# Order of the last row sums and a middle result in PSUM, in a two-layer decoder trunk on one core

## The chip, the core and the metric

The kernel runs on one core of a Trainium2 chip. The time is that of the device in microseconds (us), the median over runs of the whole kernel. The engines are named as in the profile: PE (TensorE), DVE (VectorE), ACT (ScalarE), POOL (GpSimd) and SP (SyncE, which here only issues DMAs).

## The reference, cut to what matters

```python
# 512 tokens of 1024 numbers, 2 layers; all in float32
for i in range(2):
    m = short_conv_mixer(x, ...) if i == 0 else chunked_sgu_mixer(x, ...)
    x = layer_norm(ALPHA * x + m, ln_mix_g[i], ln_mix_b[i])
    f = grouped_moe(x, ...)          # 16 experts, 2 for each token, both from one group of 4
    x = layer_norm(ALPHA * x + f, ln_ffn_g[i], ln_ffn_b[i])

def layer_norm(x, g, b):             # over the 1024 numbers of a token
    mu, var = mean(x), mean((x - mu) ** 2)
    return (x - mu) * rsqrt(var + 1e-5) * g + b
```

The change lies in the last two lines of the second layer: the sum of a token's own row with its two expert rows, and the norm of that sum, which is the output. A small part of it is in the routing of both layers, where the tokens of each expert are counted.

## The kernel before, in words

**Tiles.** The 512 tokens stand as four tiles of 128 tokens (`t` = 0 to 3), one token to a partition, 1024 numbers along it. `X[:, t, :]` in SBUF holds a tile. PSUM has 8 banks of 512 float32 numbers a partition (`ps[:, bank, :]`), so a tile takes two banks. `SB[1] = (2, 4, 0, 6)` names the first of the two banks in which the sums of tiles 0 to 3 are built in the second layer; `summed(t)` is the pair of them.

**Experts.** Each of 16 experts gets up to 112 token rows. The weights stream from HBM all the time; ACT and DVE split each into a rounded part `hi` (L466) and a rest `lo` (L477), and PE multiplies in three passes (L481 to L483). The outputs of the first 14 experts are scattered to a table `y_rows` in HBM by an indirect DMA that POOL issues (L556). The table has two halves, one for each of a token's two experts. When it is written, POOL issues for tiles 1 to 3 a DMA that adds the first half's rows to `X` (L959, semaphore `first_in`), and, as each of these lands, one that adds the second half's rows (L963, semaphore `second_in`). Tile 0 is read by SP and added by DVE.

**The last two experts** don't go through the table. Their outputs stay in SBUF, as `y_last` (two experts, a `hi` and a `lo` part each), and PE brings each row to its token by a product with a one-hot matrix `hotT`. `sum_half(1, t, h)` (L2086) does it for half `h` (512 numbers) of tile `t`: 4 products, so 8 for a tile. `own_rows(t, h)` (L2099) then adds `X`'s own rows to the same bank, by a product with the identity in full float32; the trace shows each call as two products, so 4 for a tile. It needs `second_in[t]`, since `X` is complete only then. Before the change PE works tile by tile: the one-hot products of the tile, the wait for its `second_in`, its own rows. Each call of `own_rows` raises `sum_ready`.

**The norm of a tile** (tiles 1 to 3) on DVE: two `bn_stats` from PSUM (L1638), each after its half's `sum_ready`; `bn_aggr` for mean and variance (L1360); `(sum - mean) * gain` from PSUM to `X` (L1366); the reciprocal `rstd` of the root that ACT took meanwhile (L1370). For tiles 0 to 2 DVE stops there: ACT multiplies `X` by `rstd` (L1204), POOL adds the bias (L984), and SP sends the tile out (L876). For tile 3, the last, DVE itself does `X * rstd + bias` in two halves (L1378); ACT sends the first half out (L1225), SP the second (L878). DVE's instructions run in the order in which they are written, tile after tile, and so do those of PE, ACT, POOL and SP.

**The counts.** `counts(layer)` (L1904) sums the tokens of each expert into 16 columns of PSUM bank `LGB[layer]`, which is 4 in the first layer and 2 in the second; `route_most` (L1466) takes the largest. Every engine reads it later, and runs further rounds of all experts only if it is over 112.

Of the kernel before, what the change touches and what calls it, by code (L numbers as in the profile page):

```python
# [33 lines left out]
AX = mybir.AxisListType  # L34
# [4 lines left out]
NT = S // P  # L39
KD = D // P  # L40
BANK = 512
E = 16
# [125 lines left out]
def hybrid_decoder(nc, x, x_t, w_dense0, w_moe, w_dense1, conv_w, router_w, router_bias,  # L168
                   w_s, b_s, v_gain, v_bias, ln_par, out):
    ctx = ExitStack()  # L170
    with ctx:
# [24 lines left out]
        X = place("X", [P, NT, D], F32, 80 * KB)  # L196
# [18 lines left out]
        ffn_par = [place(f"ffn_par{l}", [P, 2, D], F32, o) for l, o in ((0, 72 * KB), (1, 40 * KB))]  # L215
# [31 lines left out]
        ones_b = place("ones_b", [P, P], BF16)  # L247
# [28 lines left out]
        rstd = place("rstd", [P, NT], F32)  # L276
# [9 lines left out]
        sel = place("sel", [P, NT, E], BF16, bsb_at)  # L286
# [45 lines left out]
        scr = [scratch(0), scratch(1)]  # L332

        ps = ctx.enter_context(nc.psum_tensor("ps", [P, 8, BANK], F32))
# [152 lines left out]
        TRF = (2, 4, 0, 0)  # L487
        SB = ((2, 4, 0, 2), (2, 4, 0, 6))
        LGB = (4, 2)
        IDA = (7, 3)  # L490
        NA = 3

# [786 lines left out]
        def _(dve):  # L1279
            chain = Chain(dve, dve_step)  # L1280
# [79 lines left out]
                nc.vector.bn_aggr(mv[:, t, :], stats[:, :, :].rearrange("p a b -> p (a b)")).then_inc(var_ready, 1)  # L1360
                dve.wait_ge(var_ready, q + 1)

            def norm(q, t, par, n_par, last_step=True, src=None, parts=1):

                dve.wait_ge(par_in, 32 * n_par)
                chain.step(nc.vector.scalar_tensor_tensor(out=X[:, t, :], in0=X[:, t, :] if src is None else src,  # L1366
                                                          scalar=mv[:, t, 0:1], in1=par[:, 0, :],
                                                          op0=ALU.subtract, op1=ALU.mult))
                dve.wait_ge(std_ready, q + 1)
                ins = nc.vector.reciprocal(rstd[:, t:t + 1], std[:, t:t + 1])  # L1370
                if not last_step:
                    ins.then_inc(rooted, 1)
                    return
                chain.step(ins)
                n = D // parts
                for c in range(parts):
                    cols = slice(c * n, (c + 1) * n)
                    nc.vector.scalar_tensor_tensor(out=X[:, t, cols], in0=X[:, t, cols], scalar=rstd[:, t:t + 1],  # L1378
                                                   in1=par[:, 1, cols], op0=ALU.mult, op1=ALU.add).then_inc(normed, 1)

            def mixed(layer, t):
# [81 lines left out]
            def route_most(layer):  # L1463

                dve.wait_ge(cnt_ready, layer + 1)
                chain.step(nc.vector.reduce_max(scr[layer]["most_f"][:, :], ps[:, LGB[layer], 192:192 + E], axis=AX.X))  # L1466
                nc.vector.tensor_copy(most[:, layer:layer + 1], scr[layer]["most_f"][:, :]).then_inc(most_ready, 1)

            def route_gates(layer):
# [129 lines left out]
            def combine(layer):  # L1599

                def x_lo(t):
                    for h in range(2):
                        dve.wait_ge(xt_hi, 4 + 2 * t + h + 1)
                        dst = slice(4 * h, 4 * h + 4), slice(t * P, (t + 1) * P)
                        nc.vector.tensor_tensor(xT_lo[:, dst[0], dst[1]],
                                                ps[:, TRF[t] + h, :].rearrange("p (k s) -> p k s", k=4),
                                                xT_hi[:, dst[0], dst[1]], ALU.subtract).then_inc(xt_lo, 1)

                def summed(t):

                    return ps[:, SB[layer][t]:SB[layer][t] + 2, :].rearrange("p b n -> p (b n)")

                def first_tile():
                    for h in range(2):
                        cols = slice(h * BANK, (h + 1) * BANK)
                        dve.wait_ge(sum_ready, SUMS[0] * layer + h + 1)
                        ins = nc.vector.tensor_tensor(X[:, 0, cols], X[:, 0, cols], ps[:, SB[layer][0] + h, :], ALU.add)
                        if h == 0:
                            chain.step(ins)
                        else:  # L1620
                            ins.then_inc(sum_taken, 1)
                            dve.wait_ge(sum_taken, NT * layer + 1)
                        chain.post(nc.vector.bn_stats(stats[:, h, :], X[:, 0, cols]))
                    mean_var(8 * layer + 4, 0)

                def add_sum(t):
                    if t == 1:
                        dve.wait_ge(tile1_added, 1)
                    else:
                        dve.wait_ge(second_in[t], 16)  # L1630
                    dve.wait_ge(sum_ready, t + 2)
                    nc.vector.tensor_tensor(X[:, t, :], X[:, t, :], summed(t), ALU.add).then_inc(sum_taken, 1)
                    dve.wait_ge(sum_taken, t + 1)

                def moments_of_sum(t):
                    for h in range(2):
                        dve.wait_ge(sum_ready, SUMS[0] + 2 * t + h + 1)
                        chain.post(nc.vector.bn_stats(stats[:, h, :], ps[:, SB[1][t] + h, :]))  # L1638
                    mean_var(8 + 4 + t, t)

                first_tile()
                if layer == 1:
                    norm(8 + 4, 0, ffn_par[1], 4, last_step=False)
                    for t in range(1, NT):
                        moments_of_sum(t)
                        norm(8 + 4 + t, t, ffn_par[1], 4, last_step=t == NT - 1, src=summed(t), parts=2)
                else:
                    norm(4, 0, ffn_par[0], 2, parts=2)
                    x_lo(0)
                    own_lo(V0 + 2)  # L1650
                    add_sum(1)
                    for k in range(3, 6):
                        own_lo(V0 + k)
                    moments(5, 1)
                    own_lo(V0 + 6)
                    norm(5, 1, ffn_par[0], 2)
                    own_lo(V0 + 7)
                    x_lo(1)
                    add_sum(2)
                    moments(6, 2)  # L1660
                    norm(6, 2, ffn_par[0], 2)
                    add_sum(3)
                    moments(7, 3)
                    x_lo(2)
                    norm(7, 3, ffn_par[0], 2)
                    x_lo(3)
# [19 lines left out]
            for t in range(NT):  # L1686
                ins = nc.vector.bn_aggr(mv[:, t, :], v_parts[:, t, :, :].rearrange("p a b -> p (a b)"))
# [66 lines left out]
        def _(pe):  # L1754
# [146 lines left out]
            def counts(layer):  # L1901

                for u in range(NT):
                    ins = nc.tensor.matmul(ps[:, LGB[layer], 192:192 + E], ones_b[:, :], sel[:, u, :],  # L1904
                                           start=(u == 0), stop=(u == NT - 1))
                ins.then_inc(cnt_ready, 1)

# [174 lines left out]
            def sum_half(layer, t, h, lasts=(0, 1), last=True):  # L2082

                for q in lasts:
                    for part in range(2):
                        ins = nc.tensor.matmul(ps[:, SB[layer][t] + h, :], hotT[layer][0:T, q, t * P:(t + 1) * P],  # L2086
                                               y_last[layer][q][part][0:T, h * BANK:(h + 1) * BANK],
                                               start=(q == 0 and part == 0),
                                               stop=(last and q == 1 and part == 1))
                return ins  # L2090
# [11 lines left out]
            def sums_and_overflow(layer, soon):  # L2102

                load = heavy(pe, layer)
                pe.wait_ge(yl_lo_ready, 3 * layer + 1)
                sum_half(layer, 0, 0, (0,))
                pe.wait_ge(yl_lo_ready, 3 * layer + 2)
                sum_half(layer, 0, 0, (1,)).then_inc(sum_ready, 1)
                sum_half(layer, 0, 1, (0,))
                pe.wait_ge(yl_lo_ready, 3 * layer + 3)  # L2110
                sum_half(layer, 0, 1, (1,)).then_inc(sum_ready, 1)
                overflow_pe(pe, layer, load, soon, sum_by_slot, sum_half)
                if layer == 0:
                    for t in (1, 2):
                        sum_of(0, t).then_inc(sum_ready, 1)
                    return
                for t in range(1, NT):
                    for h in range(2):
                        sum_half(1, t, h, last=False)
                    pe.wait_ge(second_in[t], 16 if t == 1 else 16 * 2)  # L2120
                    for h in range(2):
                        own_rows(t, h).then_inc(sum_ready, 1)
# [170 lines left out]
```

## Time and profile before

| | |
|---|---|
| median of 3 runs | 1126.11 us (1125.99 to 1126.21) |
| the profiled execution | 1129.59 us |
| its span (first to last event of the core) | 1127.8 us |
| PE busy | 1104.9 us, 98% of the span |
| DVE busy | 830.3 us, 74% |
| ACT busy | 652.2 us, 58% |
| POOL busy | 119.1 us, 11% |
| PE's granted clock, whole execution | 0.997 of full speed |

The span is what the trace covers; the 1.8 us between it and the execution's own time lie around it. A profiled execution takes some 3.5 us longer than the runs without a profile. Starts in the rows below are us from the start of the span, so 1127.8 is the end. The last 20 us of the span are what the change touches.

### The profile page before, as it was taken

What the parts mean: (1) busy time and instruction counts of PE and PEld (TensorE: products, weight loads), DVE (VectorE), ACT (ScalarE), POOL (GpSimd) and SP (SyncE); (2) the same over time, 40 slices, a digit from 0 to 9 for tenths busy, and PEclk for the clock granted to TensorE, in tenths of its full rate; (3) what the DMA queues carried; (4) which work ended last, traced back from release to release, by engine and by line L of the source; (5) the groups of instructions that cost most, each with busy time, mean ns of one, the idle gap of its engine ahead of it and who ended that gap; (6) DMA issues with size and microseconds to landing.
All of it is one profiled execution on the core that took longest, in us unless ns stands there. A gap on an engine that the chain in (4) does not pass through costs nothing.

```text
span 1127.8 us, 15394 instructions
## 1 busy us (share of the span) xinstructions
PE 1104.9 (98%) x5448; PEld 871.9 (77%) x5448; DVE 830.3 (74%) x1022; ACT 652.2 (58%) x761; POOL 119.1 (11%) x104
## 2 busy tenths in 40 slices
PE   8999999899999999999999999999999999999996
PEld 7888888577777777778888888888757777777774
DVE  4553547899988999999516555535799798988996
ACT  4322323588887888853417332213558788887872
POOL 2000000031111111030000000000004111111013
PEclk9999999999999999999999999999999999999998
DMA  8925421699999999987304222440399999999986
GB/s 309 418 82 221 149 94 40 227 403 391 393 380 393 371 393 378 399 273 273 149 19 174 88 76 77 156 141 38 121 352 369 395 375 391 377 385 384 383 290 171
DMA packets 51752, 295.97 MB, mean 262 GB/s; under 512 B 8932, under 2 KB 9092, under 8 KB 22128
## 3 DMA queue, kind: packets, MB, share of 16 engines
q1 hardware_dynamic: 36096, 252.46, 58.0%
q0 software_dynamic: 9040, 20.91, 6.4%
q10 hardware_dynamic: 6560, 21.87, 5.1%
q8 instruction: 32, 0.52, 0.2%
q14 instruction: 24, 0.20, 0.0%
HBM read 277.07 MB, written 29.62 MB: 272 GB/s over the span
## 4 chain that ended last, share of the span: by engine, by line
PE 82%; DMA 10%; DVE 3%; issue 2%; ACT 1%; ACTq 0%; SPq 0%; POOL 0%; DVEq 0%; POOLq 0%
PE ps L481 24%; PE ps L483 24%; PE ps L482 24%; DMA raw_more<-in_w_moe 4%; PE ps L2046 2%; DMA raw<-in_w_dense 2%; PE ps L1963 2%; DMA X<-y_rows 1%; PE ps L1888 1%; DVE lo L477 1%; PE ps L2186 1%; PE ps L1870 1%; DMA raw<-in_w_moe 1%; PE ps L1859 1%; PE ps L1988 1%
## 5 line engine op out<-in xcount | busy, mean ns | idle before, releaser
L477 DVE TENSOR_TENSOR lo<-raw,hi 128x1024 fp32r<-128x1024 f32 x320 | 376.5, 1219 | 89.0 <-ACT hi L466 86.5
L466 ACT ACTIVATE hi<-raw 128x1024 fp32r<-128x1024 f32 x320 | 325.0, 1056 | 120.8 <-PE ps L483 80.2
L481 PE MATMUL ps<-hi,xgT_hi 128*112 128x512 f32 x480 | 190.7, 397 | 0.0
L483 PE MATMUL ps<-hi,xgT_lo 128*112 128x512 f32 x480 | 188.6, 393 | 0.0
L482 PE MATMUL ps<-lo,xgT_hi 128*112 128x512 f32 x480 | 187.9, 391 | 0.0
L477 DVE TENSOR_TENSOR lo<-raw_more,hi 128x1024 fp32r<-128x1024 f32 x128 | 153.3, 1220 | 32.9 <-ACT hi L466 30.5
L466 ACT ACTIVATE hi<-raw_more 128x1024 fp32r<-128x1024 f32 x128 | 132.8, 1057 | 56.1 <-DMA raw_more<-in_w_moe 37.1
L481 PE MATMUL ps<-xT_hi,hi 128*128 128x512 f32 x320 | 126.5, 395 | 1.4 <-DVE lo L477 1.4
L482 PE MATMUL ps<-xT_lo,hi 128*128 128x512 f32 x320 | 124.7, 390 | 0.0
L483 PE MATMUL ps<-xT_hi,lo 128*128 128x512 f32 x320 | 124.6, 389 | 0.0
L483 PEld LDWEIGHTS ps<-hi,xgT_lo 128*112 128x112 f32 x480 | 83.7, 174 | 26.5
L482 PEld LDWEIGHTS ps<-lo,xgT_hi 128*112 128x112 f32 x480 | 83.7, 174 | 25.0
L481 PEld LDWEIGHTS ps<-hi,xgT_hi 128*112 128x112 f32 x480 | 83.7, 174 | 24.9 <-issue 0.2
L481 PE MATMUL ps<-hi,hT_hi 128*112 128x512 f32 x240 | 96.2, 401 | 0.7 <-ACT hotT L992 0.7
L483 PE MATMUL ps<-hi,hT_lo 128*112 128x512 f32 x240 | 94.5, 394 | 0.0
L482 PE MATMUL ps<-lo,hT_hi 128*112 128x512 f32 x240 | 93.8, 391 | 0.0
L481 PE MATMUL ps<-hi,xT_hi 128*128 128x512 f32 x192 | 75.8, 395 | 0.0
L482 PE MATMUL ps<-lo,xT_hi 128*128 128x512 f32 x192 | 74.8, 390 | 0.0
L483 PE MATMUL ps<-hi,xT_lo 128*128 128x512 f32 x192 | 74.8, 390 | 0.0
L545 POOL DMA_INDIRECT xg<-x_rows,idx x30 | 50.2, 1672 | 233.1 <-PE ps L1963 156.0
L481 PEld LDWEIGHTS ps<-xT_hi,hi 128*128 128x128 f32 x320 | 60.1, 188 | 14.0 <-DVE lo L477 1.6
L483 PEld LDWEIGHTS ps<-xT_hi,lo 128*128 128x128 f32 x320 | 60.1, 188 | 12.6
(216 smaller groups left out, 1490.0 us busy)
## 6 DMA issues: line engine op xcount, KB each, us to landing
raw<-in_w_moe SPq DMA_DIRECT2D x128, 1024.0 KB, 12.7
raw_more<-in_w_moe SPq DMA_DIRECT2D x64, 1024.0 KB
raw<-in_w_dense SPq DMA_DIRECT2D x39, 1024.0 KB, 5.6
y_rows<-X ACTq DMA_DIRECT2D x4, 2048.0 KB, 25.3
X<-y_rows POOLq DMA_DIRECT2D x10, 512.0 KB, 9.2
x_rows<-X ACTq DMA_DIRECT2D x8, 512.0 KB, 2.6
Y<-y_rows SPq DMA_DIRECT2D x6, 512.0 KB, 5.5
xT_raw<-in_x_t SPq DMA_DIRECT2D x4, 512.0 KB, 6.5
```

Source lines behind the costliest of these rows:

```text
L466: nc.scalar.activation(hi[:, s, :], flat(raw_units(n)), ACT.Copy).then_inc(hi_ready, 1)
L477: eng.tensor_tensor(lo[:, s, :], flat(raw_units(n)), hi[:, s, :], ALU.subtract).then_inc(lo_ready, 1)
L481: nc.tensor.matmul(out_, a_hi, b_hi, start=first, stop=False)
L482: nc.tensor.matmul(out_, a_hi, b_lo, start=False, stop=False)
L483: return nc.tensor.matmul(out_, a_lo, b_hi, start=False, stop=last)
L545: return pool.indirect_dma_start(out=xg[0:T, half, :], out_offset=None, in_=x_rows[:, :], in_offset=bass.IndirectOffsetOnAxis(ap=col, axis=0),
L1859: ins = nc.tensor.transpose(ps[:, bank + h, k * P:(k + 1) * P], X[:, t, (4 * h + k) * P:(4 * h + k + 1) * P], ident[:, :])
L1870: ins = nc.tensor.matmul(ps[:, LGB[layer], P:P + E], xTt[layer][:, k, :], rw2[layer][:, k, :], start=(k == 0), stop=(k == KD - 1))
L1888: ins = nc.tensor.matmul(ps[:, 5 + k // 4, (k % 4) * P:(k % 4) * P + T], X[:, t, k * P:(k + 1) * P], scr[layer]["hot0"][:, t, :], start=(t ...
L1963: ins = nc.tensor.transpose(ps[:, 5 + k // 4, (k % 4) * P:(k % 4) * P + T], xg[0:T, c % 2, k * P:(k + 1) * P], ident[0:T, 0:T])
L1988: ins = nc.tensor.transpose(ps[:, 4, k * P:k * P + T], hid[0:T, k * P:(k + 1) * P], ident[0:T, 0:T])
L2046: return nc.tensor.matmul(ps[0:T, h, :], x0[:, k, 0:T], flat(raw_units(n))[:, h * F:(h + 1) * F], start=(k == 0), stop=(k == GU - 1))
```

## The change

Three edits. The one-hot products of tiles 1, 2 and 3 are all issued before the first wait for `second_in`, and the own rows of the three tiles follow. In the norm of the last tile, `(sum - mean) * gain` goes back to PSUM, over the sum it was made from, instead of to `X`, and the last step reads it there. The counts go to bank 2 in both layers.

```diff
+        CNT = 2
...
-            def norm(q, t, par, n_par, last_step=True, src=None, parts=1):
+            def norm(q, t, par, n_par, last_step=True, src=None, parts=1, mid=None):
 
                 dve.wait_ge(par_in, 32 * n_par)
-                chain.step(nc.vector.scalar_tensor_tensor(out=X[:, t, :], in0=X[:, t, :] if src is None else src,
+                mid = X[:, t, :] if mid is None else mid
+                chain.step(nc.vector.scalar_tensor_tensor(out=mid, in0=X[:, t, :] if src is None else src,
                                                           scalar=mv[:, t, 0:1], in1=par[:, 0, :],
                                                           op0=ALU.subtract, op1=ALU.mult))
...
-                    nc.vector.scalar_tensor_tensor(out=X[:, t, cols], in0=X[:, t, cols], scalar=rstd[:, t:t + 1],
+                    nc.vector.scalar_tensor_tensor(out=X[:, t, cols], in0=mid[:, cols], scalar=rstd[:, t:t + 1],
                                                    in1=par[:, 1, cols], op0=ALU.mult, op1=ALU.add).then_inc(normed, 1)
...
-                chain.step(nc.vector.reduce_max(scr[layer]["most_f"][:, :], ps[:, LGB[layer], 192:192 + E], axis=AX.X))
+                chain.step(nc.vector.reduce_max(scr[layer]["most_f"][:, :], ps[:, CNT, 192:192 + E], axis=AX.X))
...
-                        norm(8 + 4 + t, t, ffn_par[1], 4, last_step=t == NT - 1, src=summed(t), parts=2)
+                        norm(8 + 4 + t, t, ffn_par[1], 4, last_step=t == NT - 1, src=summed(t), parts=2,
+                             mid=summed(t) if t == NT - 1 else None)
...
-                    ins = nc.tensor.matmul(ps[:, LGB[layer], 192:192 + E], ones_b[:, :], sel[:, u, :],
+                    ins = nc.tensor.matmul(ps[:, CNT, 192:192 + E], ones_b[:, :], sel[:, u, :],
                                            start=(u == 0), stop=(u == NT - 1))
...
                 for t in range(1, NT):
                     for h in range(2):
                         sum_half(1, t, h, last=False)
+                for t in range(1, NT):
                     pe.wait_ge(second_in[t], 16 if t == 1 else 16 * 2)
                     for h in range(2):
                         own_rows(t, h).then_inc(sum_ready, 1)
```

On PE, at the very end of the program, these rows stood between the last one-hot products of tile 1 and those of tile 2 before (`y_last_1` is expert 15, `y_last_0` expert 14; the waits stand in brackets):

```order
L2086 MATMUL ps<-y_last_1_hi,hotT_97 128x512
L2086 MATMUL ps<-y_last_1_lo,hotT_97 128x512
L2099 MATMUL ps<-X,ident 128x512 [waits second_in1]
L2099 MATMUL ps<-X,ident 128x512
L2086 MATMUL ps<-y_last_0_hi,hotT_97 128x512
L2086 MATMUL ps<-y_last_0_lo,hotT_97 128x512
```

And now the program ends in the last one-hot products, those of tile 3, followed by all own rows (line numbers are 3 higher):

```order
L2089 MATMUL ps<-y_last_1_hi,hotT_97 128x512
L2089 MATMUL ps<-y_last_1_lo,hotT_97 128x512
L2102 MATMUL ps<-X,ident 128x512 [waits second_in1]
L2102 MATMUL ps<-X,ident 128x512
L2102 MATMUL ps<-X,ident 128x512 [waits second_in2]
L2102 MATMUL ps<-X,ident 128x512
L2102 MATMUL ps<-X,ident 128x512 [waits second_in3]
L2102 MATMUL ps<-X,ident 128x512
```

Sixteen one-hot products, those of tiles 2 and 3, have moved ahead of the own rows of tile 1. On DVE the last norm read and wrote so before:

```order
L1366 SCALAR_TENSOR_TENSOR X<-ps,mv,ffn_par_70 128x1024 [waits par_in,var_ready]
L1370 RECIPROCAL rstd<-std 128x1 [waits std_ready,dve_step]
L1378 SCALAR_TENSOR_TENSOR X<-X,rstd,ffn_par_70 128x512 [waits dve_step]
L1378 SCALAR_TENSOR_TENSOR X<-X,rstd,ffn_par_70 128x512
```

And so now:

```order
L1368 SCALAR_TENSOR_TENSOR ps<-ps,mv,ffn_par_70 128x1024 [waits par_in,var_ready]
L1372 RECIPROCAL rstd<-std 128x1 [waits std_ready,dve_step]
L1380 SCALAR_TENSOR_TENSOR X<-ps,rstd,ffn_par_70 128x512 [waits dve_step]
L1380 SCALAR_TENSOR_TENSOR X<-ps,rstd,ffn_par_70 128x512
```

No instruction of DVE has moved; the output of the first has, and the first input of the last two.

## Rows read from the trace of the kernel before

**Rows 1.** Page, the chain that ended last, as shares of the span by engine.

```profile
PE 82%; DMA 10%; DVE 3%; issue 2%; ACT 1%; ACTq 0%; SPq 0%; POOL 0%; DVEq 0%; POOLq 0%
```

**Rows 2.** The chain in order of time, last 27 us: start, length, what.

```profile
1101.02 8.01 DMA X<-y_rows
...
1109.07 1.98 PE ps L2099 x4
1111.06 1.83 PE ps L2086 x8
1112.89 1.72 PE ps L2099 x4
...
1120.69 1.64 DVE X L1378
```

**Rows 3.** Timeline of PE, its end: start, length, instruction, [idle before, releaser].

```profile
1108.29 0.39 PE L2086 MATMUL ps<-y_last_lo,hotT 112*128 112x512 f32 x1
...
1112.73 1.88 PE L2099 MATMUL ps<-X,ident 128*128 128x512 f32 x4
...
1116.28 1.88 PE L2099 MATMUL ps<-X,ident 128*128 128x512 f32 x4
```

**Rows 4.** Timeline of DVE over the norms of tiles 1 to 3.

```profile
1110.22 0.17 DVE L1370 RECIPROCAL rstd<-std 128x1 f32<-128x1 f32 x1
1110.30 1.50 DVE L1638 BATCH_NORM_STATS2 stats<-ps 128x6 f32<-128x512 f32 x2
...
1113.39 0.16 DVE L1370 RECIPROCAL rstd<-std 128x1 f32<-128x1 f32 x1
1113.79 0.70 DVE L1638 BATCH_NORM_STATS2 stats<-ps 128x6 f32<-128x512 f32 x1 [0.23 <-PE ps L2099]
1114.64 0.70 DVE L1638 BATCH_NORM_STATS2 stats<-ps 128x6 f32<-128x512 f32 x1 [0.16 <-PE ps L2099]
...
1115.62 1.28 DVE L1366 SCALAR_TENSOR_TENSOR X<-ps,mv,ffn_par 128x1024 f32<-128x1024 f32 x1
1116.94 0.16 DVE L1370 RECIPROCAL rstd<-std 128x1 f32<-128x1 f32 x1
...
1120.49 0.16 DVE L1370 RECIPROCAL rstd<-std 128x1 f32<-128x1 f32 x1
1120.69 2.30 DVE L1378 SCALAR_TENSOR_TENSOR X<-X,rstd,ffn_par 128x512 f32<-128x512 f32 x2
```

**Rows 5.** Timeline of POOL, same stretch: the issues of the second additions, the bias.

```profile
1104.32 0.86 POOL L963 DMA_DIRECT2D X<-y_rows  x1 [2.44 <-DMA X<-y_rows]
1106.85 0.86 POOL L963 DMA_DIRECT2D X<-y_rows  x1 [1.67 <-DMA X<-y_rows]
1114.78 7.00 POOL L984 TENSOR_TENSOR X<-X,ffn_par 128x1024 f32<-128x1024 f32 x3 [7.08 <-ACT X L1204]
```

**Rows 6.** The three DMAs of L963 in this stretch, issue to landing.

```profile
DMA to landing us min/median/max: 7.5/7.7/8.0
```

**Rows 7.** Timeline of ACT: the scaling of tile 2.

```profile
1117.14 1.15 ACT L1204 ACTIVATE X<-X,rstd 128x1024 f32<-128x1024 f32 x1 [1.22 <-DVE rstd L1370]
```

**Rows 8.** Timeline of SP, the issues of the output.

```profile
1117.19 4.95 SPq L876 DMA_DIRECT2D out<-X  x3
1123.02 0.33 SPq L878 DMA_DIRECT2D out<-X  x1
```

**Rows 9.** First layer, timelines of POOL and DVE, where both work on SBUF.

```profile
502.64 2.38 POOL L970 TENSOR_TENSOR X<-X,Y 128x1024 f32<-128x1024 f32 x1
...
502.86 3.25 DVE L1366 SCALAR_TENSOR_TENSOR X<-X,mv,ffn_par 128x1024 f32<-128x1024 f32 x1
...
506.34 1.42 DVE L1378 SCALAR_TENSOR_TENSOR X<-X,rstd,ffn_par 128x512 f32<-128x512 f32 x2
```

**Rows 10.** Groups by line and form: busy, mean ns; idle before, releaser.

```profile
L1366 DVE SCALAR_TENSOR_TENSOR X<-X,mv,ffn_par 128x1024 f32<-128x1024 f32 x1 | 1.3, 1285 | 0.0
L976 POOL DMA_DIRECT2D bsb<-in_b_s x1 | 0.6, 574 | 7.9 <-issue 7.9
```

## The prediction

> **What bounds the kernel now.** I read the chain by engine first: PE holds 82% of it [rows 1]. But the change touches only the last 20 us, so the question is which engine ends those, and for that I read the chain in order of time over the last stretch. It goes from the DMA that adds tile 1's second half of the table (issued at 1101.02, 8.01 us long, landed at 1109.03) to PE, which stays on it: own rows, one-hot products, own rows [rows 2]; then it passes through DVE's last norm and ends in L1378. The timelines say how tight that is. PE's last one-hot product of tile 1 starts at 1108.29 [rows 3]; 8 of them take 1.83 us [rows 2], 0.229 us each, so PE is free at 1108.52 and waits until 1109.07, 0.55 us. From there PE needs 3.55 us for a tile (own rows at 1112.73 and at 1116.28 [rows 3]). DVE is a little faster. When its input is there, as for tile 1, it takes 3.09 us from the first `bn_stats` (1110.30) to the start of the reciprocal (1113.39), and the next tile's `bn_stats` can start 0.08 us behind that (1110.22 to 1110.30) [rows 4]: 3.17 us a tile. The reader should see that PE wins over DVE by only 0.38 us a tile, and that DVE's waits for PE are 0.23 and 0.16 us for tile 2 [rows 4].
>
> **The order of the products.** Nothing is added or removed on PE; 16 products move ahead of tile 1's own rows. Own rows of tile 1 now start at 1108.29 + 17 x 0.229 = 1112.18, where they started at 1109.07: 3.11 us later. The data no longer decides. PE's whole work ends earlier, by what it waited: own rows take 1.72 us a tile [rows 2], so those of tiles 2 and 3 start at 1113.90 and 1115.62, the last 0.66 us before 1116.28. Their data is there: issues at 1104.32 and 1106.85 [rows 5] plus 7.7 us, at most 8.0 [rows 6], give 1112.0 to 1112.3 and 1114.5 to 1114.9.
>
> What is late next is DVE, which has three norms to do and can't start the first. For tile 2 before, the two `bn_stats` began 1.06 and 1.91 us after the own rows began (1112.73 to 1113.79 and 1114.64) [rows 3, 4]. So for tile 1 now: 1113.24 and 1114.09. From the second `bn_stats` to L1366 it takes 0.98, to the reciprocal 1.32 more (1114.64, 1115.62, 1116.94 [rows 4]): reciprocal of tile 1 at 1116.39. From here DVE's input is always ready (tile 2's second half at 1113.90 + 1.91 = 1115.81) and DVE runs at its own pace. Tile 2: `bn_stats` 1116.47, reciprocal 1119.56. Tile 3: `bn_stats` 1119.64, reciprocal 1122.73, and 0.20 us on (1120.49 to 1120.69 [rows 4]) the last step, at 1122.93. It was at 1120.69: +2.24 us.
>
> **The middle result in PSUM.** The pair of L1378 took 2.30 us, its first half 1.64 [rows 2, 4]. The same pair in the first layer, with POOL idle, took 1.42 [rows 9]. In the second layer POOL's three additions run from 1114.78 to 1121.78 [rows 5], and the first half ends at 1122.33, 0.55 us behind them. The first layer shows the same: L1366 out of SBUF, 1.28 us when alone [rows 10], takes 3.25 beside POOL's addition that ends at 505.02 [rows 9]. But L1366 with its input in PSUM takes 1.28 at 1115.62, in the middle of POOL's additions [rows 4, 5]. So a DVE instruction with two SBUF tensors waits for POOL, one with a single SBUF tensor doesn't. The Trainium skill says why ("SBUF — State Buffer", section on SBUF's two sides): an exclusive lock on a shared port pair, held for a whole instruction, which DVE needs for two SBUF inputs. By that rule the edited L1378 can't be blocked, and the trace agrees.
>
> I take 1.42 us for the new pair, so it ends at 1124.35, where it ended at 1122.99. Bounds: 1.28, what one instruction of 1024 numbers takes, to 2.30, as now. One rule of the skill speaks against it ("VectorE: DVE Perf Modes", the section on the TRN2 errata): a PSUM source costs VectorE 62 cycles more than an SBUF source. Rows of 1024 numbers don't show it, 1.284 us out of PSUM as out of SBUF [rows 4, 10]; by the rule, two halves would cost some 0.13 us more (an estimate from the page) and the sum would be 1127.6.
>
> The edited L1366 writes to PSUM, which no DVE instruction of this trace does. Bounds: a gain is excluded, since it stays one pass over 1024 numbers, so 1.28 at best; twice that, 2.57, if reading and writing the same banks took turns. I take 1.28, the row with the same inputs.
>
> **POOL and the output.** POOL's additions begin at 1114.78 though the first scaled tile is ready some 3 us earlier. I lay that on POOL's own instruction stream: in the first layer it is idle 7.9 us at the same place of its program, with no releaser [rows 10], here 7.08 [rows 5]. It stays. The next two follow the reciprocals: 0.20 us to ACT's scaling, which takes 1.15 (1116.94, 1117.14 [rows 4, 7]), then 2.33 for POOL's addition (7.00 / 3). Tile 1: 1117.78 to 1120.11. Tile 2: 1120.95 to 1123.28. SP sends tile 2 then, 1.5 us later than now (third issue of L876, about 1121.8 [rows 8]), but still 1 us ahead of the last half. So the last half of tile 3 remains the end: issued at about 1124.38 instead of 1123.02 [rows 8], with the same 4.8 us behind it.
>
> **The counts.** 4 products and one reduction a layer, unchanged but for the bank: nothing. In the first layer the old place, columns 192 to 207 of bank 4, lies under the transposes of the first expert's hidden rows, which come before the reduction; so the first layer's maximum was not a count, and now it is. Over 112 it would start further rounds of experts. The reference's routing with its inputs, worked out, gives at most 75 tokens to an expert in the first layer and 79 in the second. No rounds.
>
> **Sum.** +2.24 for the later start, -0.88 for the pair (2.30 to 1.42): +1.36 us. The profiled execution would go from 1129.59 to 1130.95; the runs without a profile are 3.48 us lower, 1126.11 to 1127.47, that is 1127.5. Without the PSUM edit the reorder alone would give about +1.5, since POOL ends at 1123.28 and holds the first half only a little (to 1123.83, the second to 1124.5). So in this order PSUM is worth only about 0.15 us, where in the old order it would have been worth 0.88.
>
> **Rivals.**
> - PE sets the end, as the chain says: DVE follows PE's 0.66 us gain and the pair gives 0.88. 1126.11 - 1.54 = 1124.6. For it: PE's place in the chain. Against it: the 3.11 us for which DVE has no input, against a lead of PE over DVE of 0.38 us a tile. 4 in 100.
> - Without a profile the table's DMA lands later beside PE. If tile 1's rows land at 1112.2 or later, 3.1 us behind this trace, nothing is delayed, and the order gains: before, the last `bn_stats` ended 9.86 us behind the landing (1116.28 + 1.91 + 0.70 - 1109.03), now it would be 8.96 (1.91 + 0.98 + 1.32 + 0.08 + 3.09 + 0.08 + 1.50). The pair gains nothing then, as POOL has long enough before it in either kernel. 1125.2; the break-even is a landing 2.2 us later. For it: landings of a chain of three DMAs, 7.5 to 8.0 us for one kind [rows 6]. Against: 0.22 us between all three runs. 11 in 100.
> - Writing to PSUM in place costs double: L1366 of tile 3 +1.28. 1128.8, slower by 0.24%. It decides "slower" from 0.9 us on. For it: same banks read and written, no row. Against: out of and into the same place in SBUF costs nothing extra [rows 10]. 10 in 100.
> - The PSUM source doesn't free DVE from POOL (the change doesn't do what it says): first half until 1123.83. 1127.6. Against: L1366 [rows 4]. 8 in 100.
> - First-layer rounds of experts through a true count: hundreds of us. 1 in 100.
>
> **How the numbers follow.** The forecast has 66 in 100, with its own range of 1126.9 to 1128.1, from a landing half a us off and a pair of 1.28 to 1.6. The 8-in-10 range reaches down to the late landing, 1125.2, and up nearly to the double write, 1128.6. About 0.2%, 2.25 us, is what a measurement of this kernel can tell from no change; the forecast, +0.12%, is inside it. Slower by more: most of the double write, the rounds and some of the forecast's tail, 16 in 100. Faster by more, below 1123.9: only the two fast rivals, both short of it, 4 in 100. Between: 80.
>
> **What would show it.** In the timeline after: own rows of tile 1 at about 1112.2 with no wait; DVE idle some 2.8 us before tile 1's `bn_stats`; no idle time before those of tile 3; the pair at about 1122.9 and 1.4 us long while POOL adds; L1368 of tile 3 at 1.28. The forecast is wrong if DVE still waits for PE at tile 3, if that L1368 is much above 1.3, or if own rows of tile 1 wait for their DMA.

## The result and the profile after

The changed kernel takes 1129.43 us (median of 22 runs, 1128.27 to 1132.71), the kernel before, run beside it, 1126.85 (22 runs, 1124.88 to 1130.42). The ratio is 1.0024, with a 95% interval of 1.0018 to 1.003: slower by 2.0 to 3.4 us. The forecast was 1127.5, +1.36 us; the range ended at 1128.6. The direction was right, the size was half of what was measured.

The two profiled execution times are alike (1129.59 before, 1129.42 after; both spans are 1127.8), because what comes before the change ran 1.4 us faster in the one of after. So I compare the ends from a common mark ahead of both edits at the end of the program (the edit of the counts lies before it, and e4 tries it alone): the start of DVE's last `y_last_lo`, the last input of the one-hot products. It is 1105.23 before. The timeline of DVE after the change begins there:

```profile
1103.86 0.75 DVE L1564 SCALAR_TENSOR_TENSOR y_last_lo<-ps,slot_gate,y_last_hi 112x512 fp32r<-112x512 f32 x1 [2.00 <-ACT y_last_hi L1154]
...
1108.85 0.16 DVE L1372 RECIPROCAL rstd<-std 128x1 f32<-128x1 f32 x1
1111.84 0.70 DVE L1640 BATCH_NORM_STATS2 stats<-ps 128x6 f32<-128x512 f32 x1 [2.83 <-PE ps L2102]
1112.70 0.70 DVE L1640 BATCH_NORM_STATS2 stats<-ps 128x6 f32<-128x512 f32 x1 [0.16 <-PE ps L2102]
...
1114.99 0.16 DVE L1372 RECIPROCAL rstd<-std 128x1 f32<-128x1 f32 x1
1115.07 1.28 DVE L1640 BATCH_NORM_STATS2 stats<-ps 128x6 f32<-128x512 f32 x2
...
1117.95 0.16 DVE L1372 RECIPROCAL rstd<-std 128x1 f32<-128x1 f32 x1
1118.03 1.28 DVE L1640 BATCH_NORM_STATS2 stats<-ps 128x6 f32<-128x512 f32 x2
...
1119.58 1.29 DVE L1368 SCALAR_TENSOR_TENSOR ps<-ps,mv,ffn_par 128x1024 f32<-128x1024 f32 x1
1120.91 0.16 DVE L1372 RECIPROCAL rstd<-std 128x1 f32<-128x1 f32 x1
1121.11 1.41 DVE L1380 SCALAR_TENSOR_TENSOR X<-ps,rstd,ffn_par 128x512 f32<-128x512 f32 x2
```

These answer to [rows 4]. DVE stands idle for 2.83 us before tile 1, where it had no wait; no idle time before tiles 2 and 3; the norm that writes to PSUM takes 1.29 us, the pair that reads it 1.41. PE, in answer to [rows 3], has no gap: its timeline ends in one block of own rows.

```profile
1110.55 0.39 PE L2089 MATMUL ps<-y_last_lo,hotT 112*128 112x512 f32 x1
1110.78 5.31 PE L2102 MATMUL ps<-X,ident 128*128 128x512 f32 x12
```

POOL, in answer to [rows 5], now adds one tile at a time, each behind its scaling:

```profile
1110.40 2.35 POOL L985 TENSOR_TENSOR X<-X,ffn_par 128x1024 f32<-128x1024 f32 x1 [5.48 <-ACT X L1205]
1116.42 2.35 POOL L985 TENSOR_TENSOR X<-X,ffn_par 128x1024 f32<-128x1024 f32 x1 [3.67 <-ACT X L1205]
1119.37 2.34 POOL L985 TENSOR_TENSOR X<-X,ffn_par 128x1024 f32<-128x1024 f32 x1 [0.61 <-ACT X L1205]
```

And SP's issues, in answer to [rows 8]. The last is 5.25 us ahead of the end of the span; before it was 4.78:

```profile
1112.78 9.29 SPq L877 DMA_DIRECT2D out<-X  x3
1122.55 0.33 SPq L879 DMA_DIRECT2D out<-X  x1
```

So the steps of the forecast are in the trace, each within half a us, and yet the kernel lost twice what was forecast. Two things were hidden: what a usual execution of the kernel before looks like, and what ends the program.

### The profile page after: what moved, and what is told of

It reads as the page before. It is cut to its first block, busy times and chain, and to the rows that moved or that the text cites. A ratio compares the mean times of both kernels' runs of the same rounds, so it can differ in the third digit from the quotient of the medians.

```text
span 1127.8 us, 15394 instructions
## 1 busy us (share of the span) xinstructions
PE 1103.2 (98%) x5448; PEld 872.3 (77%) x5448; DVE 829.6 (74%) x1022; ACT 651.8 (58%) x761; POOL 115.0 (10%) x104
## 4 chain that ended last, share of the span: by engine, by line
PE 95%; DMA 2%; DVE 2%; ACT 1%; issue 0%; SPq 0%; DVEq 0%; ACTq 0%
PE ps L481 28%; PE ps L483 28%; PE ps L482 27%; PE ps L2049 2%; PE ps L1966 2%; DMA raw<-in_w_dense 2%; PE ps L1891 1%; PE ps L2190 1%; PE ps L1873 1%; PE ps L1991 1%; PE ps L1862 1%; PE ps L2089 1%; ACT hi L466 0%; PE ps L1914 0%; DVE stats L1640 0%
## 5 line engine op out<-in xcount | busy, mean ns | idle before, releaser
L482 PEld LDWEIGHTS ps<-xT_lo,hi 128*128 128x128 f32 x320 | 60.1, 188 | 12.2 <-issue 0.2
```

The source lines that it names most:

```text
L482: nc.tensor.matmul(out_, a_hi, b_lo, start=False, stop=False)
```

## The experiments

Each kernel was timed in 5 rounds against the kernel before, but for the two repeats e10 and e11 (one round). Ratios carry their 95% interval; 0.001 is 1.13 us.

**First set: the kernel before once more, and each edit alone.** e1 is `before` unchanged. e2 is:

```diff
                     for h in range(2):
                         sum_half(1, t, h, last=False)
+                for t in range(1, NT):
                     pe.wait_ge(second_in[t], 16 if t == 1 else 16 * 2)
```

e3 is the edit of `norm` and its `mid=summed(t)` alone, e4 the edit of the bank of the counts alone (`CNT = 2`).

> The kernel before, unchanged, profiled a second time and timed against itself. Theory (the profiled execution of before was untypical at its end): POOL's three bias additions start when the scaled tiles are ready rather than together at the end, the third ends about when L1378 starts, and the pair of L1378 takes about 1.4 us instead of 2.3; with it the end of the chain from the last y_last_lo (1105.23 before) to the last output issue is about 17 us instead of 17.8. Rival (the cost of 1.2 us more than forecast lies elsewhere, in the bank of the counts or upstream): the second profile shows the same end as the first, pair of 2.3 us. Ratio to before 1.000 within 0.0005.

> Only the order of the products is changed; middle result in X and counts as before. Theory: nearly the whole loss is here, +2.3 to +2.9 us (0.21 to 0.26%), and the pair of L1378 in it takes 1.4 to 1.9 us beside POOL's third addition. Rival (the prediction's own sum, with loss elsewhere): +1.5 us (0.13%).

> Only the middle result of the last norm goes to PSUM; old order, counts as before. Theory: POOL does not hold L1378 in a usual execution, so it gains 0 to 0.3 us. The prediction's sum: a gain of 0.88 us (0.08%), as in its profiled execution. Rival (something in the PSUM edit costs): +0.5 us or more.

> Only the bank of the counts is changed, to bank 2 in both layers. Theory: 0 within 0.3 us. Rival (the missing 1.2 us lies here): +1.2 us (0.11%), and the profile shows longer waits around the first layer's first expert.

Measured: e1 1.0004 (0.9995 to 1.0014), e2 1.0027 (1.0018 to 1.0036), e3 1.0000 (0.9991 to 1.0008), e4 0.9998 (0.9989 to 1.0007). The whole loss is in the order, where the prediction gave +1.5 us for the order alone and e2 shows +3.0 (2.0 to 4.1); the counts and PSUM give nothing that can be measured. The second profile of the kernel before shows why PSUM doesn't. Its timeline of DVE, the last two steps:

```profile
1117.83 0.16 DVE L1370 RECIPROCAL rstd<-std 128x1 f32<-128x1 f32 x1
1118.03 1.42 DVE L1378 SCALAR_TENSOR_TENSOR X<-X,rstd,ffn_par 128x512 f32<-128x512 f32 x2
```

of PE, where tile 1's own rows start with no wait (the first profile had one of 0.55 us [rows 2, 3]):

```profile
1106.29 0.39 PE L2086 MATMUL ps<-y_last_lo,hotT 112*128 112x512 f32 x1
1106.52 1.88 PE L2099 MATMUL ps<-X,ident 128*128 128x512 f32 x4
```

and of POOL:

```profile
1110.25 4.74 POOL L984 TENSOR_TENSOR X<-X,ffn_par 128x1024 f32<-128x1024 f32 x2 [5.86 <-ACT X L1204]
1115.72 2.34 POOL L984 TENSOR_TENSOR X<-X,ffn_par 128x1024 f32<-128x1024 f32 x1 [0.73 <-ACT X L1204]
```

POOL's first addition starts 7.00 us behind the mark (1103.25 here), against 9.55 in [rows 5]; the third ends at 1118.06, just as L1378 starts, and the pair takes 1.42 us instead of 2.30. The last output issue stands 16.22 us behind the mark, where e1's expectation had about 17. That the pair was held by POOL in [rows 4, 5] is right, but it was a matter of that execution. e2 shows the hold at its size in the new order: 1.82 us for the pair out of SBUF, where the changed kernel has 1.41. Even there PSUM buys no time: the spans of e2 and of the changed kernel end 23.87 and 23.94 us behind the mark.

**Second set: fewer products ahead, and a gap filled.** e5 and e6 move 8 and 4 of the 16 products. e7 keeps the order before, but issues four products of tile 1 in PE's wait for the last part of `y_last`:

```diff
                 sum_half(layer, 0, 1, (0,))
+                if layer == 1:
+                    sum_half(1, 1, 0, last=False)
                 pe.wait_ge(yl_lo_ready, 3 * layer + 3)
```

> Only the 8 one-hot products of tile 2 go ahead of tile 1's own rows; tile 3's stay where they were. Middle result in X, counts as before. Theory (two lines, PE's and DVE's, and the later one sets the end): PE's last own rows end as before, DVE starts tile 1 1.83 us later and then needs 2.96 us a tile, so L1378 starts +0.5 to +0.8 us against the second profile of before (10.3 to 10.6 us behind tile 0's reciprocal, where that profile has 9.80 and 16 products ahead 12.26); the time +0.5 to +0.8 us. Rival (each product moved costs its own length): +1.8 us.

> Only 4 one-hot products, those of tile 2's first half, go ahead of tile 1's own rows. Theory: DVE starts tile 1 0.9 us later and has made it up by tile 3, where PE's last own rows set the end again: L1378 starts 9.8 us behind tile 0's reciprocal as in the second profile of before, DVE still waits 0.2 us for PE before tile 3's statistics, time within 0.3 us of before. Rival (each product moved costs its own length): +0.9 us.

> Order as before but for 4 one-hot products of tile 1's first half, which go ahead of the wait for the last part of y_last (PE idles there, and the next products start slowly: 5 products take 1.67 us in the second profile of before, where 5 others take 1.15). Theory: PE sets the end in this order, so filling its wait brings the end forward by 0.4 to 0.5 us (L1378 at 9.3 to 9.5 us behind tile 0's reciprocal, unless that is late too). Rival (tile 1's rows land too late, or tile 0's second half, now 0.3 us later, delays DVE): no gain, 0 to +0.3 us.

Measured: e5 1.0010 (1.0002 to 1.0019), e6 0.9998 (0.9989 to 1.0007), e7 1.0003 (0.9994 to 1.0011). L1378 starts 14.80 us behind the mark in e6, 14.78 in the second profile of before, 15.40 in e5, 17.25 with all 16 moved. So the delay of L1378 is that of a race: nothing while DVE makes up its late start (2.96 us a tile against PE's 3.55), then the whole of each further product. The time of e5 was expected to follow L1378, which is 0.62 us late, at +0.5 to +0.8 us; the ratio gives +1.1 (0.2 to 2.1), and its span ends 1.22 us later than e1's. In e7 L1378 starts at 14.27, 0.51 earlier as expected, but the span ends only 0.10 us earlier than e1's (20.75 and 20.85 behind the mark); the pair takes 1.68 us beside POOL's third addition. The ratio, +0.3 us (-0.7 to +1.2), can't exclude the gain of 0.4 to 0.5 that was expected. This was a first sign, not a proof, that the last norm doesn't set the end.

**Third set: what stands behind the last issue.** e8 is e7 with the PSUM edit; e9 is the changed kernel without tile 2's output; e10 and e11 repeat the changed kernel and the kernel before.

```diff
                 sp.wait_ge(normed_p, t + 1)
-                sp.dma_start(out[t * P:(t + 1) * P, :], X[:, t, :]).then_inc(out_done, 16)
+                if t < 2:
+                    sp.dma_start(out[t * P:(t + 1) * P, :], X[:, t, :]).then_inc(out_done, 16)
```

> The gap-filling order of e7 with the middle result of the last norm in PSUM. Theory: in e7 L1378 starts 0.5 us earlier but runs into POOL's third addition (1.68 us instead of 1.42); in PSUM it takes 1.41, so the last output issue comes 15.7 us behind the last y_last_lo (15.97 in e7, 16.22 in the second profile of before). Time 0.3 to 0.5 us under before, hardly to be told from no change. Rival (the outputs then land in a bunch, as after the change, and take it back): the last issue at 15.7 but the end 20.7 to 20.9 behind the last y_last_lo, no gain.

> The changed kernel without the output DMA of tile 2, whose rows of the output are left out; 256 KB blocks of tile 3 and tiles 0 and 1 go out as before. Theory (the 0.47 us that the changed kernel's trace has behind its last issue, 5.25 against 4.6 to 4.8, come from tile 2's 512 KB, issued 0.15 us ahead of tile 3's first half): landings of 2.6 to 2.8 us instead of 3.2, 4.6 to 4.8 us from the last issue to the end, time 0.4 to 0.6 us under the changed kernel, so +1.9 to +2.2 us over before. Rival (that profile was merely slow at its end): 4.6 to 4.8 us in the repeat of the changed kernel as well, and no difference in time.

> The changed kernel, unchanged, profiled a second time. Theory: pair of 1.41 us starting 17.2 us behind the last y_last_lo, landings of 3.2 us and some 5.2 us from the last issue to the end, as in its first profile. Rival: the end behind the last issue is 4.8 us.

> The kernel before, profiled a third time. Theory: as in its second profile, PE does not wait before tile 1's own rows (or under 0.1 us), and the pair of L1378 takes 1.4 us. Rival (both ends occur about as often): a wait of 0.4 us or more and a pair of 1.8 us or more.

Measured: e8 1.0003 (0.9994 to 1.0012), e9 1.0022 (1.0013 to 1.0032), e10 1.0020 (1.0010 to 1.0030), e11 0.9995 (0.9985 to 1.0005). My theory for e9 fell: tile 3's outputs land 2.1 us behind their issue instead of 3.2, and the span still ends 5.20 us behind the last issue. e8's expectation missed too, a last issue 15.7 us behind the mark where 16.42 was measured: in its profile PE waited again for tile 1's rows, and the filled gap was lost to the landing:

```profile
1107.03 1.98 PE L2101 MATMUL ps<-X,ident 128*128 128x512 f32 x4 [0.44 <-DMA X<-y_rows]
```

The repeat of the changed kernel is like its first profile (pair 1.41, 5.26 us behind the last issue). The third profile of before lies between the other two: no wait of PE, but POOL's first addition 8.23 us behind the mark and the pair 1.66 us long. So the rival of e11, that both ends occur, is partly right: the start of POOL's additions wanders, and with it the hold on L1378. POOL's timeline of that profile names no releaser:

```profile
1112.42 7.01 POOL L984 TENSOR_TENSOR X<-X,ffn_par 128x1024 f32<-128x1024 f32 x3 [6.75 <-issue]
```

What does stand still in all these profiles is the distance from the end of POOL's last addition to the end of the span. The rows of line 171, which hold the end of each engine's queue, tell it. A DRAIN there is a row of an engine's queue that ends no earlier than the engine's last work. In the changed kernel:

```profile
L171 POOLq DRAIN  x1: 8192/8192/8192, 1119.3 to 1119.3; - x1
L171 DVEq DRAIN  x1: 1447/1447/1447, 1121.1 to 1121.1; - x1
L171 SPq COMPARE_BRANCH  x1: 38/38/38, 1125.8 to 1125.8; - x1
...
L171 SPq EVENT_SEMAPHORE  x1: 17/17/17, 1127.7 to 1127.7; - x1
```

POOL's queue drains from 1119.3 for 8.19 us, to 1127.5; the addition ends at 1121.71, so 5.8 us of it come behind POOL's last work. The other engines have left theirs by 1126.0, and the semaphores of the end follow the drain. In us behind the mark (the mark, then the end of POOL's last addition, SP's last issue, the end of the span):

```
                     mark      POOL ends   last issue   span ends   end - POOL
before             1105.23       16.55       17.79        22.57        6.02
e1  before again   1103.25       14.81       16.22        20.85        6.04
e11 before, third  1104.19       15.24       16.48        21.31        6.07
e3  PSUM only      1103.45       14.80       16.24        20.85        6.05
e4  counts only    1104.07       14.99       16.42        21.03        6.04
e6  four ahead     1105.05       15.12       16.36        21.15        6.03
e7  gap filled     1102.95       14.74       15.97        20.75        6.01
e8  gap, PSUM      1103.68       14.99       16.42        21.02        6.03
e5  eight ahead    1103.83       16.01       17.25        22.07        6.06
e2  order only     1102.83       17.85       19.09        23.87        6.02
e9  two outputs    1103.37       17.85       18.73        23.93        6.08
e10 after again    1102.85       17.86       18.69        23.95        6.09
after              1103.86       17.85       18.69        23.94        6.09
```

The last column moves by 0.08 us over thirteen profiles; the span less the last issue moves between 4.6 and 5.3.

**Fourth set: take POOL off the end.** e12 and e13 leave out POOL's third bias addition, in the changed kernel and in the kernel before: tile 2 goes out without its bias as soon as ACT has scaled it.

```diff
-                sp.wait_ge(normed_p, t + 1)
+                sp.wait_ge(*((normed_p, t + 1) if t < 2 else (scaled, 3)))
...
+                if t == 2:
+                    continue
                 pool.wait_ge(scaled, t + 1)
```

e14 computes everything, but shares tile 2's last step: DVE does the second half, ACT and POOL only the first. e15 is e14 with e7's order and the PSUM edit.

```diff
-                nc.gpsimd.tensor_tensor(X[:, t, :], X[:, t, :], ffn_par[1][:, 1, :], ALU.add).then_inc(normed_p, 1)
+                cols = slice(0, D if t < 2 else BANK)
+                nc.gpsimd.tensor_tensor(X[:, t, cols], X[:, t, cols], ffn_par[1][:, 1, cols], ALU.add).then_inc(normed_p, 1)
...
                 if not last_step:
                     ins.then_inc(rooted, 1)
+                    if t == 2:
+                        dve.wait_ge(rooted, 3)
+                        nc.vector.scalar_tensor_tensor(out=X[:, t, BANK:D], in0=X[:, t, BANK:D], scalar=rstd[:, t:t + 1],
+                                                       in1=par[:, 1, BANK:D], op0=ALU.mult, op1=ALU.add).then_inc(half2, 1)
                     return
```

> The changed kernel without POOL's third bias addition: tile 2 of the output lacks its bias and goes out as soon as ACT has scaled it. Theory (the end of the program is set by POOL: in all 13 profiles the span ends 6.0 to 6.1 us behind POOL's last addition, of which a DRAIN on POOL's queue takes 5.85): POOL's last work ends some 3 us earlier and the outputs of tile 3 set the end, 3.0 to 3.4 us behind the last output issue; span end 21.7 to 22.1 us behind the last y_last_lo instead of 23.95, time 1.8 to 2.2 us under the changed kernel, +0.4 to +0.7 us over before. Rival (the last norm and its output set the end): end 5.2 us behind the last issue, time as the changed kernel, +2.3 to +2.6 us over before.

> The kernel before, with the same left out. Theory: span end 19.2 to 19.6 us behind the last y_last_lo instead of 20.85 to 21.3, time 1.3 to 2.0 us under before (0.12 to 0.18%); against the changed kernel with the same left out it is 2.5 us faster, which is the price of the order without POOL. Rival (the last norm and its output set the end): no change in time.

> The kernel before with tile 2's last step shared: DVE finishes its second half (rstd and bias, one instruction of 512 numbers, behind tile 2's reciprocal), ACT scales and POOL biases only the first half. Everything is computed. Theory: POOL's last addition ends 1.6 us earlier, DVE is 0.2 to 0.5 us later at tile 3; span end 19.4 to 19.8 behind the last y_last_lo, time 1.0 to 1.4 us under before (0.09 to 0.12%). Rival (the last norm sets the end): 0.2 to 0.5 us over before.

> e14 with the order of e7 and the middle result of the last norm in PSUM. Theory: another 0.3 to 0.5 us where tile 1's rows land in time, so 1.2 to 1.9 us under before (0.11 to 0.17%). Rival (the landing of tile 1's rows takes the filled gap back, as in e8): as e14.

Measured: e12 1.0000 (0.9991 to 1.0009), e13 0.9981 (0.9972 to 0.9990), e14 0.9990 (0.9981 to 0.9999), e15 0.9989 (0.9981 to 0.9998). The rival in both, that the last norm and its output set the end, would have left e12 at +2.3 us and e13 at nothing; it is refuted. By the ratios e12 is 2.7 us faster than the changed kernel, and e13 2.1 us faster than the kernel before; both gains are a little above what was expected (1.8 to 2.2 and 1.3 to 2.0). Where POOL is out of the way the outputs set the end. The order costs its price there too, through the late L1378: the span of e12 ends 2.48 us later behind the mark than that of e13 (21.25 and 18.77), and the ratios are 2.1 us apart. So taking POOL off the end wouldn't save the new order. (e12 to e15 ran on another chip than e1 to e11; the distances from the mark compare, since L1378 starts at 17.24 in e12 and 17.26 in e10, 14.79 in e13 and 14.78 in e1.) In e13, POOL, and SP's last issues:

```profile
1112.80 2.37 POOL L986 TENSOR_TENSOR X<-X,ffn_par 128x1024 f32<-128x1024 f32 x1 [0.28 <-ACT X L1206]
```

```profile
1112.54 3.63 SPq L876 DMA_DIRECT2D out<-X  x3
1119.66 0.33 SPq L878 DMA_DIRECT2D out<-X  x1
```

The span ends at 1122.2, 2.54 us behind that issue (2.57 in e12, where 3.0 to 3.4 were expected), and the outputs land 2.1 us behind theirs. In e14 POOL's last addition is a half one and ends at 1116.97, 6.03 us ahead of the end, so POOL still sets it, 1.4 us earlier than in e1:

```profile
1110.49 4.82 POOL L988 TENSOR_TENSOR X<-X,ffn_par 128x1024 f32<-128x1024 f32 x2 [5.82 <-ACT X L1209]
1115.61 1.36 POOL L988 TENSOR_TENSOR X<-X,ffn_par 128x512 f32<-128x512 f32 x1 [0.30 <-ACT X L1209]
```

All fifteen profiles and the two of the comparison fit one line within 0.1 us: the end is the later of POOL's last addition + 6.0 and the last output issue + 2.55. The second term is the later one only in e12 and e13, where the landing takes 2.1 us, so it rests on these two. By it e14 stands at 19.4 and 19.3, so nearly balanced. e14 and e15 beat both kernels of the comparison, by about 1.2 us against before; e15's gap was again lost to the landing of tile 1's rows (PE waits 0.44 us for it in its profile), so of e15 over e14 nothing is shown.

## Why the prediction was wrong in size

**What bounds the kernel now: the step that failed.** The last 20 us as a contest of PE and DVE were read rightly as far as L1378. The reading stopped there: the prediction took tile 3's last half as the end, carried the 4.8 us behind SP's last issue [rows 8] along as a constant, and set POOL aside. They were no constant: 4.6 to 5.3 us in thirteen profiles, 2.54 and 2.57 where POOL's last addition is left out. What is constant is POOL's last addition + 6.0. The chain of the kernel before ends in DVE's own drain, 4.8 us short of the end of the span; POOL's, in the rows of line 171, which I had not read, lasts to 1127.57. The last line of that chain, and POOL's row:

```profile
1122.33 0.66 DVEq L171
L171 POOLq DRAIN  x1: 9271/9271/9271, 1118.3 to 1118.3; - x1
```

In the sum, +2.24 for L1378 should have been POOL's 2.6 to 3.05 us (below), and -0.88 for the pair should have been nothing.

**The order of the products: right in mechanism.** Forecast: tile 1's `bn_stats` 8.01 us behind the mark (1113.24), measured 7.98; no wait at tiles 2 and 3, measured none. L1378 was forecast at 17.70 (1122.93), measured 17.25: the 3.17 us a tile contained a wait of 0.2 us between the two `bn_stats` of tile 1 (1.50 us for two [rows 4], 1.28 where both inputs are ready), so DVE's own pace is 2.96. Against a usual execution of before (14.78) the delay is 2.47 us, against 2.24 in the forecast.

**The middle result in PSUM: the hold was real, its -0.88 was not.** The pair takes 1.41 us (forecast 1.42), the norm that writes to PSUM 1.29 (forecast 1.28; the rival of a double price is out). But the 2.30 us it was set against belong to one execution in which POOL started late; in the next two the pair takes 1.42 and 1.66, so the pair itself could gain 0 to 0.25 us. As a term of the time the -0.88 measured nothing, 0.0 (-1.0 to +0.9) in e3, because the pair isn't what ends the program. The trace of after agrees with the Trainium skill's rule of the exclusive lock ("SBUF — State Buffer", SBUF's two sides): with one SBUF input the pair is 1.41 us while POOL adds until 1121.71, with two it is 1.82 in e2 for the same overlap of 0.6 us. The 62 cycles more for a PSUM source that the Trainium skill states ("VectorE: DVE Perf Modes", the TRN2 errata) didn't show: 1.41 us out of PSUM, 1.42 out of SBUF.

**POOL and the output: the number right, its part in the end missed.** The prediction had POOL's last addition right (end at 1123.28, 18.05 behind the mark; measured 17.85) and then set it aside, since SP would send tile 2 ahead of tile 3's last half. It is POOL's own end that counts, as e12 and e13 show. The change moves tile 2's reciprocal, from 11.04 us behind the mark in e1 to 14.09; ACT and POOL follow it. So the price is 3.05 us against an execution like e1, and less where POOL starts late anyhow: 17.85 - 15.24 = 2.6 against e11, 1.3 against the profile of the forecast. The forecast's +1.36 and the +1.37 between the two first profiles (22.57, 23.94) agree by chance: in the first profile POOL's last addition ended 1.74 us later than in e1, and the pair of L1378 1.56 us later. The measured 2.0 to 3.4 us lie around the price against e1 and e11.

**The base.** That profile was 1.3 to 1.7 us longer behind the mark than the next two of the same kernel. The prediction said a profiled execution lies 3.5 us over the runs and took the difference as an offset; a third to a half of it was the very stretch under study, and e1's profiled execution, at 1125.76 us, isn't longer than its runs (median 1126.52). The clue was there: POOL was idle for 7.08 us, until 3.2 us behind the scaling of tile 0, the only one that its first addition waits for (ended at 1111.57); the releaser named in [rows 5] fits tile 1's scaling, which ended at 1114.74, and only by its time.

**The rivals.** PE as the end: no. The late landing, by which the change would have gained 0.9 us: no. Of the ten profiles in which tile 1's products alone stand ahead of its own rows, PE doesn't wait for the landing in six (e1, e3, e7, e11, e13, e14), under 0.1 us in one (e4) and 0.4 to 0.6 us in three (before, e8, e15). A hold in spite of PSUM: no. A true count in the first layer: e4 shows no rounds.

**Still open.** Why POOL's drain lasts 5.8 us behind its last work, and why its first addition starts 5.1 to 7.1 us behind its last DMA issue, sometimes with the scaled tile long ready. No experiment here changed either.

## What to carry to other kernels

Read what stands between the last work of each engine and the end of the span, drains of the queues included, before calling a chain critical: here POOL's last addition + 6.0 us ended the program, 2.1 us (before) and 2.7 us (after) later than the last norm and its output did once that addition was left out. When an early wait is filled with later work, ask what starts from the first result: a 0.55 us wait of PE was filled with 3.7 us of products, and DVE, ACT and POOL, which had run beside PE, all started late. And before a gain of under a us is read from one profile, look whether the piece is the same in a second.

## What the runs showed of the hardware

- A DRAIN on POOL's queue at the program's end finishes 5.8 us behind POOL's last addition (5.77 to 5.85 in 17 profiles), whether that has 1024 numbers a partition (the DRAIN itself lasts 8.19 us in after) or 512 (7.17 and 7.22 in e15 and e14). Where POOL ends last, the span ends 0.2 to 0.3 us later.
- DVE writing 1024 float32 numbers a partition to PSUM, over its own input, takes 1.29 us (after, L1368); from PSUM to SBUF 1.28.
- The outputs of tile 3 land 2.1 us behind their issue where tile 2's 512 KB aren't sent (e9) or go out over 2 us ahead (e12, e13), 3.2 us where these are issued 0.15 us ahead (after), 2.6 to 2.8 us in the kernel before (before, e1, e11).
